# Adaptive modulation vectors: column sums as two rows and a DMA round trip in place of transposes and reductions

## The reference

```
cond = silu(c)                                  # 1024 values
m = cond @ ada_w[layer] + ada_b[layer]          # 1024 x 6144 weights, two layers
shift1, scale1, gate1, shift2, scale2, gate2 = split(m, 6)      # 1024 values each
h = rmsnorm(x, norm1_g) * (1 + scale1) + shift1
x = x + gate1 * attention(h)
h = rmsnorm(x, norm2_g) * (1 + scale2) + shift2
x = x + gate2 * swiglu(h)
```

## Time and profile before

| | before |
|---|---|
| median of 3 runs | 1173.44 us (1173.38 to 1174.34) |
| profiled execution, whole time | 1174.04 us |
| its span | 1172.2 us |
| PE busy | 1160.1 us, 99% |
| DVE busy | 820.6 us, 70% |
| ACT busy | 599.3 us, 51% |
| POOL busy | 51.1 us, 4% |
| mean granted TensorE clock | 0.999 of full speed |
| DMA traffic | 253.66 MB |

### The profile page before, as it was taken

The page is one execution under the profiler, slowest core; times in us unless marked ns, Lnnn a source line. Parts: engine busy times, 40 slices in busy tenths (PEclk is TensorE's granted clock), DMA queues, the critical chain, the costliest instruction groups (busy, mean ns, idle before and its releaser), DMA issues. The chain is left out here.

```text
span 1172.2 us, 15112 instructions
## 1 busy us (share of the span) xinstructions
PE 1160.1 (99%) x6140; PEld 978.5 (83%) x6140; DVE 820.6 (70%) x1051; ACT 599.3 (51%) x780; POOL 51.1 (4%) x101
## 2 busy tenths in 40 slices
PE   8999999999999999999999999999999999999998
PEld 6888888889989888888888888888888978888887
DVE  5777877456757657887898967788785658554544
ACT  7443356445566643353578544334565676433441
POOL 0011110000000001111000001111000000000000
PEclk9999999999999999999999999999999999999999
DMA  9888684554445578887624457887546405755530
GB/s 370 340 307 320 222 346 179 198 182 143 144 145 166 194 269 318 298 289 277 248 72 145 180 215 271 298 319 270 224 144 235 143 20 196 251 179 179 184 139 37
DMA packets 44421, 253.66 MB, mean 216 GB/s; under 512 B 5568, under 2 KB 5952, under 8 KB 20544
## 3 DMA queue, kind: packets, MB, share of 16 engines
q1 hardware_dynamic: 29088, 199.78, 46.9%
q0 software_dynamic: 13824, 50.34, 12.1%
q10 hardware_dynamic: 1440, 2.58, 0.6%
HBM read 251.63 MB, written 1.05 MB: 216 GB/s over the span
## 5 line engine op out<-in xcount | busy, mean ns | idle before, releaser
L1094 DVE TENSOR_TENSOR w_lo<-raw,w_hi 128x2048 fp32r<-128x2048 f32 x145 | 330.8, 2288 | 101.0 <-ACT w_hi L465 100.9
L465 ACT ACTIVATE w_hi<-raw 128x2048 fp32r<-128x2048 f32 x145 | 275.3, 1911 | 32.8 <-DMA raw<-in_w 32.6
L1885 PE MATMUL ps<-w_hi,h_parts 128*128 128x512 f32 (+1 forms) x720 | 284.2, 395 | 1.0 <-DVE h_parts L1218 0.5
L1887 PE MATMUL ps<-w_lo,h_parts 128*128 128x512 f32 (+1 forms) x720 | 277.8, 386 | 0.0
L1886 PE MATMUL ps<-w_hi,h_parts 128*128 128x512 f32 (+1 forms) x720 | 277.3, 385 | 0.0
L542 ACT ACTIVATE hid_hi<-ps 128x512 fp32r<-128x512 f32 (+1 forms) x48 | 27.0, 562 | 260.3 <-PE ps L2010 260.3
L1885 PEld LDWEIGHTS ps<-w_hi,h_parts 128*128 128x128 f32 x720 | 135.5, 188 | 27.7 <-DVE h_parts L1229 0.9
L1887 PEld LDWEIGHTS ps<-w_lo,h_parts 128*128 128x128 f32 x720 | 135.3, 188 | 27.9
L1886 PEld LDWEIGHTS ps<-w_hi,h_parts 128*128 128x128 f32 x720 | 135.8, 189 | 25.0
L1109 DVE SCALAR_TENSOR_TENSOR ada_acc<-ada_raw,cond,ada_acc 128x1024 f32<-128x1024 f32 x84 | 107.5, 1280 | 3.4 <-DMA ada_raw<-in_ada_w 1.2
L1094 DVE TENSOR_TENSOR lo_extra<-raw_extra,hi_extra 128x2048 fp32r<-128x2048 f32 x40 | 91.5, 2287 | 13.6 <-ACT hi_extra L465 13.5
(11 more groups left out here) (236 smaller groups left out, 1686.7 us busy)
## 6 DMA issues: line engine op xcount, KB each, us to landing
raw<-in_w SPq DMA_DIRECT2D x146, 1024.0 KB, 4.9
ada_raw<-in_ada_w POOLq DMA_DIRECT2D x96, 512.0 KB, 5.2
raw_extra<-in_w SPq DMA_DIRECT2D x40, 1024.0 KB, 5.1
raw<-in_w SPq DMA_DIRECT2D x4, 256.0 KB, 5.9
gate<-in_ada_b ACTq DMA_DIRECT2D x2, 512.0 KB, 12.3
gate<-in_ada_b SPq DMA_DIRECT2D x2, 512.0 KB, 5.9
out_x<-x SPq DMA_DIRECT2D x4, 256.0 KB, 2.0
const<-in_const ACTq DMA_DIRECT2D x1, 768.0 KB, 8.1
```

The source lines that it names most:

```text
L465: act.activation(w_hi[SLOT[u]], raw[SLOT[u]], ACT.Copy).then_inc(hi_ready, 1)
L1094: V.tensor_tensor(w_lo[SLOT[u]], raw[SLOT[u]], w_hi[SLOT[u]].bitcast(F32), ALU.subtract) \
L1885: TE.matmul(dst, x_hi, wh, start=start, stop=False, skip_group_check=True)
L1887: return TE.matmul(dst, x_hi, wl, start=False, stop=last, skip_group_check=True)
```

## The change

Each part now has one job, not two, and takes the path below; `MOD_JOBS` has 12 entries (pairs 4, 6 and 8 of stages 0, 1 and 2, pair 2 of stages 1, 2 and 3).

1. PE, end of pair `p`: two float32 matmuls with a 128x64 all-ones matrix as stationary operand, over the two 512-column halves of `ada_acc`, into partitions 0 to 63 and 64 to 127 of PSUM bank 3. All 64 rows of a half are equal; two of the 128 rows carry the 1024 sums.
2. ACT, end of pair `p` (`send_mod`): copies the 128x512 bank to `mod_row`, waits for that copy, and starts a transfer of rows 0 and 64 to a line of a scratch tensor in memory.
3. ACT, pair `p + 1`, after its first weight unit and ahead of `silu` (`fetch_mod`): waits until that transfer has landed, then starts another: for a gate, the 1024 values spread to all 128 partitions; for a shift or scale, eight rows of 128 values.
4. Shift or scale: PE, end of pair `p + 1`, waits for that transfer and turns the 8x128 rows to 128x8 with one transpose. DVE adds the bias, and for a scale the gain is folded in. Gate: DVE adds the 128x1024 rows to `gate`, with no PSUM read and no PE work.

The high and low copies of the gate sums, the all-ones fp32r matrix and the 128x512 reductions are gone.

```diff
-    for _half in range(2):
-        MOD_JOBS[(PAIRS * _f + 4 + 2 * _i if _i < 3 else PAIRS * (_f + 1) + 2) + _half] = (_q, _half)
+    MOD_JOBS[PAIRS * _f + 4 + 2 * _i if _i < 3 else PAIRS * (_f + 1) + 2] = _q
...
+                def send_mod(q):
+                    act.wait_ge(mod_ps, q + 1)
+                    wait(act, mod_sent, 16 * q)
+                    act.activation(mod_row[:, :], ps[:, 3, :], ACT.Copy).then_inc(mod_copied, 1)
+                    act.wait_ge(mod_copied, q + 1)
+                    act.dma_start(scratch[q].rearrange("(s n) -> s n", s=2), mod_row[0:P:P // 2, :]).then_inc(mod_sent, 16)
+
+                def fetch_mod(q):
+                    act.wait_ge(mod_sent, 16 * (q + 1))
+                    layer, kind = q // 6, q % 6
+                    if kind in GATE:
+                        act.dma_start(gate_rows[:, :], scratch[q].partition_broadcast(P)).then_inc(mod_in, 16)
+                    else:
+                        act.dma_start(mod_lines[0:C, :], scratch[q].rearrange("(k p) -> k p", p=P)).then_inc(mod_in, 16)
+
                 def pair(p):
...
                     hi(ug + AHEAD)
+                    if f * PAIRS + p - 1 in MOD_JOBS:
+                        fetch_mod(MOD_JOBS[f * PAIRS + p - 1])
                     silu(p, 0)
                     silu(p, 1)
                     hi(ug + 1 + AHEAD)
-                    q = gate_of_pair(f * PAIRS + p)
-                    if q is not None:
-                        act.wait_ge(ada_used, C * (q + 1))
-                        act.activation(acc_hi[:, :], ada_acc[:, q % 2, :], ACT.Copy).then_inc(acc_hi_done, 1)
                     if p > 0:
                         hi(ud + AHEAD)
+                    if f * PAIRS + p in MOD_JOBS:
+                        send_mod(MOD_JOBS[f * PAIRS + p])
...
-            def mod_job(q, h):
+            def mod_job(q):
                 layer, kind = q // 6, q % 6
-                job = 2 * q + h
-                dve.wait_ge(mod_ps, job + 1)
                 if kind in GATE:
                     i = GATE.index(kind)
+                    dve.wait_ge(mod_in, 16 * (q + 1))
                     dve.wait_ge(gate_in[i], 16 * (layer + 1))
-                    V.tensor_tensor(gate[:, i, half(h)], gate[:, i, half(h)], ps[:, 3, :], ALU.add) \
-                        .then_inc(mod_read, 1)
+                    V.tensor_tensor(gate[:, i, :], gate[:, i, :], gate_rows[:, :], ALU.add).then_inc(mod_done, 1)
                     return
-                V.tensor_reduce(mod[:, layer, part], ps[:, 3, :].rearrange("p (t n) -> p t n", t=4), AX.X, ALU.add) \
-                    .then_inc(mod_read, 1)
+                dve.wait_ge(mod_turned, turned_mods(q))
+                V.tensor_tensor(mod[:, layer, part], ps[:, 3, 0:C], bias, ALU.add).then_inc(mod_done, 1)
...
-                        V.tensor_tensor(acc_lo[:, :], ada_acc[:, q % 2, :], acc_hi[:, :].bitcast(F32), ALU.subtract) \
-                            .then_inc(acc_lo_done, 1)
...
                 def mod_job(p):
+                    before = MOD_JOBS.get(f * PAIRS + p - 1)
+                    if before is not None and before % 6 not in GATE:
+                        pe.wait_ge(mod_in, 16 * (before + 1))
+                        TE.transpose(ps[:, 3, 0:C], mod_lines[0:C, :], ident[0:C, 0:C]).then_inc(mod_turned, 1)
                     if f * PAIRS + p not in MOD_JOBS:
                         return
-                    q, h = MOD_JOBS[f * PAIRS + p]
+                    q = MOD_JOBS[f * PAIRS + p]
                     pe.wait_ge(ada_used, C * (q + 1))
-                    wait(pe, mod_read, 2 * q + h)
-                    if q % 6 in GATE:
-                        pe.wait_ge(ones_set, 1)
-                        pe.wait_ge(acc_lo_done, GATES.index(q) + 1)
-                        TE.matmul(ps[:, 3, :], ones_r[:, :], acc_hi[:, half(h)], start=True, stop=False)
-                        TE.matmul(ps[:, 3, :], ones_r[:, :], acc_lo[:, half(h)], start=False, stop=True) \
-                            .then_inc(mod_ps, 1)
-                        return
-                    for k in range(4):
-                        m = TE.transpose(ps[:, 3, k * P:(k + 1) * P],
-                                         ada_acc[:, q % 2, h * HALF + k * P:h * HALF + (k + 1) * P], ident)
+                    pe.wait_ge(const_in, 16)
+                    wait(pe, mod_done, q)
+                    for h in range(2):
+                        m = TE.matmul(ps[h * HD:(h + 1) * HD, 3, :], ones[:, 0:HD], ada_acc[:, q % 2, half(h)],
+                                      start=True, stop=True, skip_group_check=True)
                     m.then_inc(mod_ps, 1)
```

More of the change, by code:

```diff
@@ L107 @@
 ADA_FROM, ADA_PAIRS = 2, 8
-GATES = [q for q in range(ADA_PARTS) if q % 6 in GATE]
 MOD_JOBS = {}
@@ L247, in program @@
         xn = overlay("xn", 56 * T, [P, 2, D])
-        acc_hi = overlay("acc_hi", 50 * T, [P, D], F32R)
-        acc_lo = overlay("acc_lo", 56 * T, [P, D], F32R)
+        gate_rows = overlay("gate_rows", 50 * T, [P, D])
+        mod_row = overlay("mod_row", 54 * T, [P, HALF])
+        mod_lines = overlay("mod_lines", 56 * T, [P, P])
+        scratch = nc.dram_tensor("mod_rows", (ADA_PARTS, D), F32).ap()
         y_tok = overlay("y_tok", 0, [P, 2, 16, HD])
@@ L296, in program @@
         hi_ready, lo_ready, unit_done = sem("hi_ready"), sem("lo_ready"), sem("unit_done")
-        ada_used, acc_hi_done, acc_lo_done, ones_set = sem("ada_used"), sem("acc_hi_done"), sem("acc_lo_done"), sem("ones_set")
+        ada_used = sem("ada_used")
         ident_in, const_in, dist_in, mask2_in = sem("ident_in"), sem("const_in"), sem("dist_in"), sem("mask2_in")
@@ L310, in program @@
         proj_out, low_out = sem("proj_out"), sem("low_out")
-        mod_ps, mod_read, mod_bias, modg_done = sem("mod_ps"), sem("mod_read"), sem("mod_bias"), sem("modg_done")
+        mod_ps, mod_copied, mod_sent, mod_in = sem("mod_ps"), sem("mod_copied"), sem("mod_sent"), sem("mod_in")
+        mod_turned, mod_done, modg_done = sem("mod_turned"), sem("mod_done"), sem("modg_done")
         up_done, value_done = sem("up_done"), sem("value_done")
@@ L367, in bank_before, with turned_mods @@
             return None if p == 0 else (p - 1, t)
+        def turned_mods(q):
+            return len([i for i in range(q + 1) if i % 6 not in GATE])
         def ada_of_pair(g):
@@ L449, in late_inputs @@
             def late_inputs():
-                act.activation(ones_r[:, :], ones, ACT.Copy).then_inc(ones_set, 1)
                 act.dma_start(const[:, C_DIST:], inp["const"][:, C_DIST:]).then_inc(dist_in, 16)
@@ L1110, in ada @@
                                            ALU.add).then_inc(ada_used, 1)
-            def mod_job(q, h):
+            def mod_job(q):
                 layer, kind = q // 6, q % 6
-                job = 2 * q + h
-                dve.wait_ge(mod_ps, job + 1)
                 if kind in GATE:
                     i = GATE.index(kind)
+                    dve.wait_ge(mod_in, 16 * (q + 1))
                     dve.wait_ge(gate_in[i], 16 * (layer + 1))
-                    V.tensor_tensor(gate[:, i, half(h)], gate[:, i, half(h)], ps[:, 3, :], ALU.add) \
-                        .then_inc(mod_read, 1)
+                    V.tensor_tensor(gate[:, i, :], gate[:, i, :], gate_rows[:, :], ALU.add).then_inc(mod_done, 1)
                     return
-                part = slice(8 * kind + 4 * h, 8 * kind + 4 * h + 4)
-                V.tensor_reduce(mod[:, layer, part], ps[:, 3, :].rearrange("p (t n) -> p t n", t=4), AX.X, ALU.add) \
-                    .then_inc(mod_read, 1)
-                dve.wait_ge(mod_read, job + 1)
+                part = slice(8 * kind, 8 * kind + 8)
                 bias = ada_bT[:, 48 * layer + part.start:48 * layer + part.stop]
-                V.tensor_tensor(mod[:, layer, part], mod[:, layer, part], bias, ALU.add).then_inc(mod_bias, 1)
-                if kind in SCALE and h == 1:
+                dve.wait_ge(mod_turned, turned_mods(q))
+                V.tensor_tensor(mod[:, layer, part], ps[:, 3, 0:C], bias, ALU.add).then_inc(mod_done, 1)
+                if kind in SCALE:
                     which = SCALE.index(kind)
-                    dve.wait_ge(mod_bias, 8 * layer + 4 * which + 4)
-                    V.scalar_tensor_tensor(mod_g[:, layer, which, :], mod[:, layer, 8 * kind:8 * kind + 8], 1.0,
+                    dve.wait_ge(mod_done, q + 1)
+                    V.scalar_tensor_tensor(mod_g[:, layer, which, :], mod[:, layer, part], 1.0,
                                            vec_t[:, 32 + 8 * layer + 16 * which:40 + 8 * layer + 16 * which], ALU.add,
@@ L1257, in modulation @@
                 def modulation(p):
-                    if f * PAIRS + p in MOD_JOBS:
-                        mod_job(*MOD_JOBS[f * PAIRS + p])
+                    if f * PAIRS + p - 1 in MOD_JOBS:
+                        mod_job(MOD_JOBS[f * PAIRS + p - 1])
                 def pair(p):
@@ L1325, in ffn @@
```

(6 more changed lines are left out.)

9 lines of the change are left out of this document (1 added, 8 removed).

## The result

The changed kernel takes 1180.41 us (median of 4 runs, 1179.69 to 1181.53), against 1173.53 us for the kernel before on the same chip: 1.0058 of it, with a 95% interval of 1.0044 to 1.0072. The forecast was 1179.2. The profiled execution took 1180.12 us, 6.08 more than that of before, and its span grew by 6.0 us.

What follows compares the result with a forecast made beforehand. PE's queue was taken as the bound: -11.4 + 14.5 + 2.6 = +5.7 us, waits costed at nothing, taking the median from 1173.44 to 1179.2 us. Range for 8 in 10: 1175.5 to 1181.8 us.

Steps and rivals of the forecast that it cites:

- The bound: Whole kernel: PE's own queue sets the end, busy 1160.1 of 1172.2 us; other engines matter only where PE waits.
- The removed groups: PE loses 16 shift or scale halves (7.4 us), eight gate halves (3.8) and a 0.25 us gap: 11.4 us.
- the 0.25 us put down to `acc_lo`: Extra gap at one gate half on PE, ascribed to `acc_lo`, which the change removes: 0.25 us saved.
- The sums: Float32 matmuls on PE: 0.85 us streaming plus 0.36 shape change, 1.21 a part; twelve parts add 14.5 us.
- The small transposes: Eight 8x128 transposes on PE for shifts and scales: 0.33 us each (0.07 to 0.50), 2.6 us added.
- the sum of +5.7: Net PE time: -11.4 removed, +14.5 for sums, +2.6 for small transposes, waits at nothing; in us.
- The waits: PE's wait for the fetch and the gates' spread cost nothing; `silu` begins perhaps 0.1 us later.
- the cover: Time spans hiding transfers: 3.5 us to spare before ACT's fetch, 4.7 us before PE's use.
- A: Rival: PE's shape change is hidden by loading weights ahead; -1.0 us, 1172.4 us; chance 0.14.
- B: Rival: the two column halves of a sum don't run together on PE; 10.2 us more, 1189.4; chance 0.03.
- C: Rival: transfers late in busy FFN stages, PE waits at `mod_in`; +7 us on top, 1186; chance 0.06.
- D: Rival: DVE and ACT, freed of work, shorten joints between stages; 1 us or so at most; no own chance.

Runs made afterwards that it cites:

- the doubled groups: The kernel before, with every modulation group of PE issued twice, same result: 1183.92 us, 1.0091 of the kernel before.
- the versions with blocks: Changed kernel, but DVE turns 32x32 blocks and adds over 32, PE folds by one 32-column matmul: 1166.63 us; direct gates 1166.11; gate addition moved later 1165.32.
- the version with one-column matmuls: Changed kernel, but shifts and scales use eight 128x128 blocks of the sum as stationary operands against one column of ones: 1182.85 us, 1.0076 of the kernel before.

## Why the prediction was right, and where it was off

**The bound.** PE's queue did set the end: DVE lost 15.5 us of work and the time rose, and the PE groups removed and added come to 6.3 us where the profiles have 6.08. The medians are 6.9 apart; the 0.8 us on top are of the size of the spread of the runs (1179.69 to 1181.53).

**The removed groups.** 11.4 us; the doubled groups gave 10.5 us in the time for some 11.2 expected, as a second copy doesn't pay the 0.03 us of a group's own (0.5 us over 16). Right, and so is the 0.25 us put down to `acc_lo`: the load of that gate's group starts 0.12 us after the end of `acc_lo` in the kernel before (158.88, 159.00) and in the doubled one (159.97, 160.09), where the group at 510.81 follows its own after 0.8 us and has no gap.

**The sums.** 1.21 forecast, 1.21 to 1.22 found. The split was 0.85 for streaming and 0.36 for the shape, and the runs divide the 1.22 in two ways. One more matmul on one half costs 0.87, which leaves 0.35 for the visit; taking 504 columns away gives 0.79 and leaves 0.43. So some 0.08 us of a visit with 8 columns is hidden, or isn't paid, beside 512 columns; which of the two isn't shown. The split of the forecast is that of the first way, and its closeness isn't luck.

**The small transposes.** 0.33 forecast, 0.38 found, the term that was mis-sized: 0.4 of the 0.6 us by which the groups exceed the sum of +5.7. I priced the shape alone and set the transpose's own time at next to nothing. The full-array transpose shows both parts: 0.12 us for a lone transpose, 0.26 for the shape. The lower value of the range was itself built from that 0.12 less its 128 columns; the passes of one column, 0.11 us each, say that these columns are not what it pays for. The rule of about 60 cycles in the Trainium skill ("TensorEngine Tiling (Array Packing)", Instruction Overhead) isn't what a lone small matmul costs here: an estimated 0.025 us against 0.38, and against 0.11 for a pass of one column on the full array.

**The waits.** No PE wait, as forecast; `silu` in its place within 0.02 us. Two steps behind it were off. The fetch is issued at 96.64, 0.5 us ahead of the arithmetic that stands before it in ACT's queue, so there was more room than the 4.7 us that I worked out: 10.8 us from issue to use, 10.2 for the tightest of the eight, where in the run with late fetches each had landed within 5.3 us of its issue. And the small write was to land in 2 to 4 us. The changed kernel's records show no landing, only that each write had landed when its fetch was issued, 5.4 to 6.0 us after it. In the versions with blocks, whose records do show it, a write took 3.7 to 7.4 us (medians 4.8 to 5.6). So the nothing for the waits was right, but the write was taken too fast and the issue of the fetch too late, two errors that point opposite ways. The risk in the cover wasn't the time of a transfer either, but that ACT's queue can stand still ahead of it.

**The rivals.** A (shape change hidden) is excluded by the 0.43 and the 0.26, and by the loads that don't run ahead. The argument against it named rows 6 too, but these show one half-array group behind another, and no full-array matmul; rows 7 and 8 alone bear on it. B (one half after the other) is excluded by 1.22 against 2.09. C (transfers late) doesn't happen in the changed kernel. Its price was also counted for three parts of the first stage, of which one is a gate and has no transpose. D gave nothing: PE's short waits at the joints are the same 0.5 us ones.

**The range.** 1175.5 to 1181.8 us was said to be the sum with the bounds of the two prices, which is 1175.3 to 1181.6. The 1180.41 lies in both.

## What to carry to other kernels

Price work on a saturated TensorE by the distance over the group between two steady matmuls, and price a change of the array's shape by itself: here 0.35 to 0.43 us for a visit to column halves and 0.26 for an operand of 8 rows, more than the few columns that it saves. Ask where in each queue the moved work lands, and behind which waits: the same 1.22 us addition was free two instructions later, and the same fetches cost some 9 us at the end of the pair, where one of them stood behind a wait for a weight unit. Work for a saturated engine is best shrunk first on one with time to spare, as the 32x32 turns and sums on VectorE did.

## What the hardware showed that I had not expected

- A load of a stationary operand for the same full-array shape starts with the matmul before it (106.91 both); for another shape it starts 0.32 us after that matmul, together with its own, and PEld sits idle for 0.35 us.
- A single wait of 2.6 us on PE was followed, some 1.2 us after its end, by some 3.4 us at a granted clock of 0.50, worth another 1.6 us: here a late transfer cost well over its own lateness. The profiled execution of the version with one-column matmuls has such a spell of 3.4 us too, in attention, after two waits of PE for ACT of about 0.5 us each.
- A float32 matmul of one column on the full array takes 0.11 us a pass, 1.81 us for 16, where 504 more columns on both halves in two passes take 0.79.
- ACT issued a transfer ahead of arithmetic that stands before it in its queue (96.64 against 97.13), but not ahead of that arithmetic's wait for a load (142.77 against 142.76).
- A 4 KB write in the busy FFN stages landed in 4.8 to 5.6 us (medians of four), a 512 KB spread to all partitions in 5.0 to 7.9; single ones took 3.7 to 7.4 and 3.4 to 9.4.
